# Where 21 sample states of an mLSTM stand among a layer's projections

## The reference

```
num   = sc v + dec (C q)            # one vector of 256 per state
C_new = dc C + (ws v) k^T           # the decayed state plus a rank-one update
h     = num / max(|den|, exp(-m))   # then gated by sigmoid(o) and normalised per head
```

## Time and profile before

| | |
|---|---|
| median of 3 runs | 1765.01 us (1763.52, 1765.01, 1767.86) |
| the profiled execution | 1766.36 us, its span 1764.2 us |
| mean granted clock of TensorE | 0.997 |
| instructions | 22648 |
| DMA | 196.23 MB, mean 111 GB/s |

### The profile page before, as it was taken

The page is one execution under the profiler, slowest core; times in us unless marked ns, Lnnn a source line. Parts: engine busy times, 40 slices in busy tenths (PEclk is TensorE's granted clock), DMA queues, the critical chain, the costliest instruction groups (busy, mean ns, idle before and its releaser), DMA issues.

```text
span 1764.2 us, 22648 instructions
## 1 busy us (share of the span) xinstructions
PE 1744.2 (99%) x8390; PEld 1361.2 (77%) x8390; DVE 869.8 (49%) x1801; ACT 592.5 (34%) x1437; POOL 499.0 (28%) x539
## 2 busy tenths in 40 slices
PE   9999999999899999999999999999999999999998
PEld 5577766988788888747658888888888888888643
DVE  1444323785566556552333444355435544466775
ACT  2321235564465234311221223432333234533312
POOL 0251100335222002410003543145414553123630
PEclk9999999999999999999999999999999999999999
DMA  7312111247655235541111111223123343745323
GB/s 270 137 61 79 53 64 57 53 135 174 200 159 173 90 93 150 176 167 48 50 48 59 47 48 44 97 90 96 50 73 117 102 141 109 270 159 167 126 104 112
DMA packets 149079, 196.23 MB, mean 111 GB/s; under 512 B 19083, under 2 KB 108171, under 8 KB 148834
## 3 DMA queue, kind: packets, MB, share of 16 engines
q1 hardware_dynamic: 140708, 174.58, 31.2%
q10 hardware_dynamic: 8262, 20.20, 3.4%
HBM read 156.97 MB, written 37.85 MB: 110 GB/s over the span
## 4 chain that ended last, share of the span: by engine, by line
PE 90%; DVE 3%; issue 3%; ACT 1%; DMA 1%; POOL 1%; DVEq 0%; SPq 0%; ACTq 0%; POOLq 0%
PE PS L3511 51%; PE PS L2257 7%; PE PS L2407 5%; PE PS L2047 3%; PE PS L396 3%; PE PS L570 3%; PE PS L2498 2%; PE PS L2083 2%; PE PS L2058 2%; PE PS L291 2%; PE PS L2080 2%; PE PS L920 1%; DVE WK L727 1%; PE PS L913 1%; PE PS L1337 1%
## 5 line engine op out<-in xcount | busy, mean ns | idle before, releaser
L3511 PE MATMUL PS<-HT,RING 128*128 128x258 f32 (+2 forms) x1776 | 444.6, 381 | 0.3 <-ACT WK L3601 0.3
L3511 PEld LDWEIGHTS PS<-HT,RING 128*128 128x128 f32 x1776 | 329.5, 190 | 46.0 <-issue 1.1
L3601 ACT ACTIVATE BIG<-PS 128x256 f32<-128x256 f32 (+2 forms) x140 | 53.8, 385 | 382.3 <-PE PS L3511 382.2
L3511 PE MATMUL PS<-BIG,RING 128*128 128x258 f32 (+1 forms) x656 | 159.6, 382 | 0.0
L3511 PEld LDWEIGHTS PS<-BIG,RING 128*128 128x128 f32 x656 | 123.1, 190 | 17.9 <-issue 0.2
L3511 PE MATMUL PS<-BIG,WK 128*128 128x258 f32 (+1 forms) x448 | 114.2, 386 | 5.2 <-DVE BIG L3703 5.2
L3511 PE MATMUL PS<-HT,CST 128*128 128x256 f32 (+2 forms) x432 | 110.2, 382 | 0.1
L3511 PEld LDWEIGHTS PS<-BIG,WK 128*128 128x128 f32 x448 | 84.3, 193 | 17.9 <-DVE BIG L3703 5.6
L3511 PEld LDWEIGHTS PS<-HT,CST 128*128 128x128 f32 x432 | 79.6, 190 | 11.5 <-DVE BIG L3700 0.9
L570 PE MATMUL PS<-WK,RING 128*128 128x344 f32 x288 | 84.3, 453 | 0.1
L3697 DVE TENSOR_TENSOR BIG<-BIG,PS 128x256 f32<-128x256 f32 (+1 forms) x70 | 29.6, 422 | 104.8 <-PE PS L3511 104.8
(11 more groups left out here) (452 smaller groups left out, 3255.5 us busy)
## 6 DMA issues: line engine op xcount, KB each, us to landing
RING<-in_w_in_a SPq DMA_DIRECT2D x14, 1024.0 KB, 6.2
WK<-in_cache_mem_kv SPq DMA_DIRECT2D x56, 256.0 KB, 5.7
RING<-in_w_kv_b SPq DMA_DIRECT2D x12, 1024.0 KB, 5.3
RING<-in_w_in_b SPq DMA_DIRECT2D x12, 1024.0 KB, 5.2
WK<-in_cache_win SPq DMA_DIRECT2D x40, 256.0 KB, 5.1
RING<-in_w_mkv SPq DMA_DIRECT2D x16, 512.0 KB, 5.1
BIG<-in_x_prompt SPq DMA_DIRECT2D x16, 512.0 KB
BIG<-sample_query SPq DMA_DIRECT2D x28, 256.0 KB, 5.7
```

What stands on the lines that cost most here:

```text
L3511: last = nc.tensor.matmul(PS[:, bank, 0:mid - lo], weight_block(u // 2, s, k), h_block(layer_of(u), u % 2, t, k), start=(k == 0 and j not ...
L3601: nc.scalar.activation(part(u, n2 if j == 0 else n1, lo, mid), PS[:, banks(u)[0], 0:mid - lo], ACT.Copy).then_inc(sig("projections_copied" ...
```

## The change

```diff
@@ -1233,9 +1233,13 @@
             at = (2 * (h % 2) + e) * W
             return WK[:, at:at + W]
 
+        def state_slot(i):
+
+            n = i - EARLY_STATES
+            return (9, 12, 16)[n] if n < 3 else 24 + 17 * (n - 3) // 5
+
         def states_at(x):
-            return [i for i in range(EARLY_STATES, H * NS)
-                    if 9 + 7 * ((i - EARLY_STATES) // 2) + 3 * (i % 2) == x]
+            return [i for i in range(EARLY_STATES, H * NS) if state_slot(i) == x]
 
         def gated(u):
 
```

## The result

The change makes the kernel slower. Beside it the kernel before took 1763.42 us (median of 6 runs, 1759.82 to 1767.86) and the changed one 1777.72 (6 runs, 1776.84 to 1778.81); the ratio is 1.0078, with a 95% interval of 1.0062 to 1.0094. The prediction said 1772, slower, with a range of 1765.5 to 1777: the sign was right, the size too small, and the measured time lies just above the range. A repetition at the end of the study gave 1777.67 against 1766.73, ratio 1.0063 (1.0049 to 1.0077).

What follows compares the result with a forecast made beforehand. TensorE, busy 99% of the span, was taken as the bound. From 1766.4 us, -8.5 + 0.6 + 4.5 + 4.8 + 2.4 gave 1770.2; one clock loss made 1773.4, and the median's 1.35 offset 1772 (range 1765.5 to 1777).

Steps and rivals of the forecast that it cites:

- The old wait: TensorE's wait before slot 22, 5.33 us, and 3.16 us of slower clock behind it would go: minus 8.5 us.
- The step on the load: State 11's load, issue untouched, lands at 451.90; its product, finished at 453.3, is ready before slots 23 and 24 want it.
- The three gates: Output gates of heads 1, 2, 3 would wait for later sums, delaying slots 38, 66, 94: plus 4.5, 4.8, 2.4 us.
- slot 31's tenths: Head 0's square root on ScalarE would end later and delay slot 31: plus 0.6 us, bounds 0 and 1.
- its 4.5 us for VectorE in slot 92: At head 3's gate, VectorE's work after ScalarE's sums at 590.9 would take 4.5 us, ending at 595.4.
- The clock: TensorE would drop to half clock once between the waits in slots 38 and 66: plus 3.2 us, bounds 0 and 6.4.
- The forecast's rival with two losses: TensorE would lose the clock behind both waits, in slots 38 and 66, giving 1775 us; chance 0.2.
- The anchor: The median of the runs before lies 1.35 us below the profiled execution of 1766.4, so the sum 1773.4 became 1772.

Runs made afterwards that it cites:

- the kernel with two waits filled: Changed kernel with eight extra matmuls, results unused, ahead of slot 38 and of slot 66, where TensorE waits; 1775.58 us.

## Why the prediction was right in its mechanism and too low in its size

**The old wait** went in full, minus 8.5, and nothing took its place in slots 22 to 24. The step on the load was right; the runs with state 11 loaded first confirm the cause.

**The three gates** came where the prediction put them, in slots 38, 66 and 94, with slot 31's tenths ahead of them. The sizes for slots 38 and 66 were too low by 0.8 and 0.5. The step that failed there took VectorE's times for the gate from the earlier trace rows as they stood. In the changed kernel the sums of states 15 and 23 release GpSimd's next product together with the gate, and VectorE is slower beside it, by 0.85 us up to the sum (3.85 for 3.00). By luck a second error hid a part of this: the forecast added busy times that overlap in the timeline, so its 4.5 us for VectorE in slot 92, where no product is left to disturb it, were 4.1 (600.92 to 605.00), and that term came out at 2.1 for 2.4.

**The clock** is the first mis-sized term: I took one loss of 3.2 for two waits, and both lost it, at 2.2 and 3.0 in the first profile, 3.1 and 1.8 in the second. The reasoning was that the spread of before's runs means that even 5.2 us does not always lose the clock; but behind every unfilled wait of 4.2 us or more in the profiles of this study, ten of them, it was lost, and 41 of the 49 later runs of before have the lower mean clock. With waits of 1.6 and 5.17 us alone, the rows of before could not say what one of 4.5 does. The forecast's rival with two losses, at 1775 and a chance of 0.2, was the case that came, 2.7 us above its own figure.

**The anchor** is the second. The sum was moved down by the 1.35 us by which the profiled execution lay above a median of three, 1765.0. But that execution began layer one at 409.5 us, the changed one at 411.7, and over 24 runs the median of before is 1766.45, not 1765.0. Three runs of a kernel whose times spread over 12 us do not fix a median to 1 us.

Together these make up the miss of 5.7 us: 2.0 by the clock, 0.9 by the gates and slot 31, 1.35 by the anchor, 2.2 by the start of layer one and 0.4 behind slot 94, less the 1.1 us by which the profiled execution (1778.81) lies above the median.

The best check of the sum is against a kernel without waits. The changed kernel stands 18.2 us above the one with state 11 loaded first (1777.7 against 1759.5); by slots its second profile loses 0.5 at slot 31, 5.3, 5.3 and 2.1 at the gates, and 3.1 and 1.8 by the clock, 18.1 in all. Of this the old wait, 1766.5 - 1759.5 = 7 us in the typical run of before, comes back, which leaves 11.2. The repetition gave 10.9; the first comparison gave 14.3, because its six runs of before had a median of 1763.42, lower than in all later series.

## What to carry to other kernels

When work is moved to a later slot to give its load time, list who waits for it, and in which slot: here one counter had readers at fixed slots, and one state three slots late for such a reader cost 7 us by slots and 9 by the medians, while the lateness of 21 states without such a reader cost 0.8 and 1.6. Before spreading work, look at the order of the queue that loads it; one load ahead of another, which waited for a store, removed the same wait with nothing moved. And price a TensorE wait of over 4 us with the slower matmuls behind it: 1.5 to 3.2 us behind each of the ten here.

## What the runs showed of the hardware that I had not expected

- A VectorE step of 0.17 us took 0.60, and two products of 2.50 us took 2.92, while GpSimd's product, released by the same semaphore, was at work; put behind it, they were back at 0.18 and 2.50.
- A TensorE wait of 1.9 us can bring the lower clock or leave it: it stayed at 1.00 in both profiles of the changed kernel (605 to 610 us in the first) and in the one with GpSimd's product moved, and fell to 0.66 over five microseconds in the kernel with two waits filled. Length alone does not decide between them.
